# Six weight slots in the in-projection rounds; x leaves the chip after the first norm and is loaded again

## The chip, the cores and the metric

The kernel runs on one core of one Trainium2 chip. The metric is the device time of one execution in microseconds (us), the median of several runs. The activations, the weights and the result are float32; large products are made of rounded high and low parts, as told below.

## The reference

One decoder layer on 256 tokens of width 2048: a norm, one wide projection (16 heads of mLSTM and retention with their gates), the heads, an output projection, and a dense feed-forward block. Cut to what matters here:

```python
h = rmsnorm(x, g_mix_pre[l])                       # (256, 2048)
proj = h @ w_in[l]                                 # w_in: 2048 x 8208
mq, mk, mv, mo, mi, mf, rq, rk, rv, rg = jnp.split(proj, SPLITS, axis=-1)
qk = jax.nn.silu(causal_dwconv(jnp.concatenate([mq, mk], axis=-1), conv_w[l], conv_b[l]))
hm = mlstm_chunkwise(...)                          # 8 heads, chunks of 128
hm = head_rmsnorm(hm, g_mlstm_head[l]) * jax.nn.sigmoid(mo)
hr = retention_chunkwise(rotary(rq), rotary(rk), rv)   # 8 heads
hr = head_rmsnorm(hr, g_ret_head[l]) * jax.nn.silu(rg)
mix = jnp.concatenate([hm, hr], axis=-1) @ w_out[l]    # 2048 x 2048
x = x + rmsnorm(mix, g_mix_post[l])
h = rmsnorm(x, g_ffn_pre[l])
ff = (jax.nn.silu(h @ w_gate[l]) * (h @ w_up[l])) @ w_down[l]   # width 5632
x = x + rmsnorm(ff, g_ffn_post[l])
```

## The kernel before

**Weights.** All weights stream through `raw`, four chunks of 1 MB (`RAW_CHUNKS`), filled by SyncE's DMA queue. A piece of 1024 columns of a chunk (a "sub"; eight subs are a "round", two subs fill a chunk) is converted by ScalarE into a rounded high part (`hi`, L711, into `w_hi`), VectorE makes the low part from the raw value and the high part (`lo`, L1132, into `w_lo`), and TensorE multiplies with both (`sub_columns`, `sub_tokens`, all through `mm` at L1787). `w_hi` and `w_lo` have `AHEAD` = 4 slots each. `more_hi` and `more_lo` are two further slots each, so that the feed-forward rounds have `FF_SLOTS` = 6. They lie in the same on-chip memory as `resid`, which holds x from the start of the kernel to the end of the output projection.

**Rounds.** Four rounds (0 to 3) make the values v. Then come twelve in-projection rounds, `R_IN` = 4 to 15. In this text they are rounds P0 to P11, and their subs are counted through, sub 0 to sub 95: P0 has subs 0 to 7, P1 has 8 to 15, P7 has 56 to 63, P8 has 64 to 71. They go in groups of three, one group for four heads: a query round, a key round (`KEY_ROUNDS`: P1, P4, P7, P10) and a gate round. During the gate round TensorE also does the heads of the group: `scores`, `weighted`, `turned`. A round has two units, each with its own pair of accumulator banks. Four output-projection rounds (`R_OUT`) follow.

**What sets the order.** The order on each engine is written out by hand. "Step n" is what ScalarE and VectorE do once TensorE has finished sub n (`sub_done`). In step n ScalarE converts sub n + 4 (`ahead`, then `hi`), and VectorE makes its low part (`lo`). Between the conversions stand the mixer's pieces (`mixer_step`, `head_step`): at the end of a unit ScalarE copies half of the accumulators into `right` (`copy_right`, L828), VectorE adds the other half (`unit_sums`, L1319), which also tells TensorE that the banks are free (`acc_free`), and then does a convolution in two halves (`convolve`, L1342 and L1346) or, in the third and fourth group, a rotation (`rotate`, L1356 to L1362). ScalarE then makes `qT` or `kT` (L867) for `scores`. VectorE's `weigh` (L1374) turns the scores into `probs` for `weighted`. Once, in P1, ScalarE also makes the decay matrices of the first eight heads (`mlstm_decay`, L818 to L822), from a row that goes through main memory by the POOL queue (`neg_all`). In most steps the conversion stands ahead of the mixer's piece; in steps 3, 5 and 7 of a key round it stands behind it on ScalarE.

**Loads.** `load` waits until VectorE has made the low parts of all subs of the chunk's former contents (`lo_done`), then issues the transfer; `raw_full` tells ScalarE of its landing. In the key rounds the source is cut so that a contiguous piece of main memory is 256 columns, 1 KB; in the other in-projection rounds it is 2 KB.

## Time and profile before

| | us |
|---|---|
| median of 3 runs (1198.7 to 1198.92) | 1198.8 |
| the profiled execution, its device time | 1198.35 |
| its span, first to last instruction | 1196.6 |

| engine | busy us | share of the span |
|---|---|---|
| TensorE (PE) | 1183.2 | 99% |
| VectorE (DVE) | 997.0 | 83% |
| ScalarE (ACT) | 690.6 | 58% |
| GpSimd (POOL) | 81.4 | 7% |

The granted TensorE clock is full in all 40 slices. The weights make 231.05 MB on SyncE's queue, whose packets take 61.9% of the 16 DMA engines' time. Read such a page from the engine that is never idle: here TensorE, so that only what makes TensorE wait, or adds work to it, moves the time. Busy times of matmuls overlap and hide short waits, so the waits are read from start times in the timeline.

### The profile page before, as it was taken

What the parts mean: (1) busy time and instruction counts of PE and PEld (TensorE: products, weight loads), DVE (VectorE), ACT (ScalarE), POOL (GpSimd) and SP (SyncE); (2) the same over time, 40 slices, a digit from 0 to 9 for tenths busy, and PEclk for the clock granted to TensorE, in tenths of its full rate; (3) what the DMA queues carried; (4) which work ended last, traced back from release to release, by engine and by line L of the source; (5) the groups of instructions that cost most, each with busy time, mean ns of one, the idle gap of its engine ahead of it and who ended that gap; (6) DMA issues with size and microseconds to landing.
All of it is one profiled execution on the core that took longest, in us unless ns stands there. A gap on an engine that the chain in (4) does not pass through costs nothing.

```text
span 1196.6 us, 16463 instructions
## 1 busy us (share of the span) xinstructions
PE 1183.2 (99%) x5727; PEld 992.7 (83%) x5727; DVE 997.0 (83%) x1334; ACT 690.6 (58%) x930; POOL 81.4 (7%) x87
## 2 busy tenths in 40 slices
PE   8999999999999999999999999999999999999997
PEld 7888888888888888888888888888888888888885
DVE  6656777877786755879999999999999789979997
ACT  5654676474654744665666566555656455555553
POOL 1000110000000000001110110111010011001100
PEclk9999999999999999999999999999999999999999
DMA  8656867767786656565575666657566765655654
GB/s 314 206 159 158 226 172 153 182 144 190 182 190 170 226 186 194 171 236 195 198 234 184 205 212 221 200 192 238 185 201 210 246 199 192 217 201 188 231 170 149
DMA packets 124596, 237.23 MB, mean 198 GB/s; under 512 B 8312, under 2 KB 24960, under 8 KB 123392
## 3 DMA queue, kind: packets, MB, share of 16 engines
q1 hardware_dynamic: 122784, 231.05, 61.9%
q0 software_dynamic: 1760, 5.51, 1.8%
q8 instruction: 30, 0.49, 0.2%
q14 instruction: 22, 0.18, 0.0%
HBM read 229.97 MB, written 4.20 MB: 196 GB/s over the span
## 4 chain that ended last, share of the span: by engine, by line
PE 92%; DVE 4%; DMA 2%; ACT 1%; issue 1%; SPq 0%; DVEq 0%; ACTq 0%
PE bank L1787 90%; DMA raw<-in_w_in 2%; DVE w_lo L1132 1%; DMA resid<-in_x 1%; PE bank L2064 1%; DVE w_lo L1618 0%; PE bank L1792 0%; PE bank L1981 0%; ACT w_hi L711 0%; DVE more_lo L1618 0%; DVE raw L1635 0%; DVE v_sb L1259 0%; DVE gT L1346 0%; DVE h L1159 0%; DVE resid L1780 0%
## 5 line engine op out<-in xcount | busy, mean ns | idle before, releaser
L1132 DVE TENSOR_TENSOR w_lo<-raw,w_hi 128x1024 fp32r<-128x1024 f32 x172 | 209.1, 1223 | 120.4 <-ACT w_hi L711 120.0
L711 ACT ACTIVATE w_hi<-raw 128x1024 fp32r<-128x1024 f32 x172 | 180.5, 1058 | 162.0 <-PE bank L1787 149.6
L1787 PE MATMUL bank<-hT,w_hi 128*128 128x512 f32 x768 | 271.1, 396 | 0.4 <-DVE w_lo L1132 0.4
L1787 PE MATMUL bank<-w_hi,h2T 128*128 128x512 f32 x778 | 253.4, 391 | 0.0
L1787 PE MATMUL bank<-hT,w_lo 128*128 128x256 f32 x768 | 214.6, 279 | 0.0
L1787 PEld LDWEIGHTS bank<-hT,w_hi 128*128 128x128 f32 x768 | 144.0, 187 | 32.7 <-DVE w_lo L1132 0.7
L1787 PEld LDWEIGHTS bank<-w_hi,h2T 128*128 128x128 f32 x778 | 146.1, 188 | 30.0
L1787 PE MATMUL bank<-w_lo,h2T 128*128 128x512 f32 x379 | 147.5, 389 | 0.0
L1787 PEld LDWEIGHTS bank<-hT,w_lo 128*128 128x128 f32 x768 | 145.0, 189 | 0.0
L1615 DVE TENSOR_TENSOR w_lo<-raw,w_hi 128x1024 fp32r<-128x1024 f32 x108 | 131.0, 1228 | 12.6 <-ACT w_hi L1022 12.5
L1618 DVE TENSOR_TENSOR w_lo<-raw,w_hi 128x1024 fp32r<-128x1024 f32 (+1 forms) x130 | 135.2, 1075 | 2.3 <-ACT w_hi L1036 1.7
L1036 ACT ACTIVATE w_hi<-raw 128x1024 fp32r<-128x1024 f32 (+1 forms) x130 | 115.8, 934 | 36.3 <-PE bank L1787 22.3
L1787 PE MATMUL bank<-w_hi,ffT 128*128 128x512 f32 x406 | 129.6, 389 | 0.0
L1022 ACT ACTIVATE w_hi<-raw 128x1024 fp32r<-128x1024 f32 x108 | 109.6, 1051 | 33.9 <-PE bank L1787 33.1
L1036 ACT ACTIVATE more_hi<-raw 128x1024 fp32r<-128x1024 f32 x78 | 74.7, 975 | 54.7 <-DVE raw L1630 45.5
L671 POOL TENSOR_TENSOR raw<-raw 128x512 f32<-128x512 f32 x43 | 60.1, 1399 | 545.6 <-DVE w_lo L1615 177.4
L1787 PEld LDWEIGHTS bank<-w_hi,ffT 128*128 128x128 f32 x406 | 76.2, 188 | 15.8
L1618 DVE TENSOR_TENSOR more_lo<-raw,more_hi 128x1024 fp32r<-128x1024 f32 x78 | 88.1, 1143 | 1.0
L1787 PE MATMUL bank<-more_hi,h2T 128*128 128x512 f32 x258 | 85.8, 389 | 0.0
L1787 PEld LDWEIGHTS bank<-w_lo,h2T 128*128 128x128 f32 x379 | 71.2, 188 | 14.5
L1787 PE MATMUL bank<-w_hi,hT 128*128 128x512 f32 x256 | 81.3, 393 | 1.0 <-DVE w_lo L1132 1.0
L1787 PE MATMUL bank<-w_hi,mixT 128*128 128x512 f32 x256 | 80.1, 391 | 0.0
(265 smaller groups left out, 1819.5 us busy)
## 6 DMA issues: line engine op xcount, KB each, us to landing
raw<-in_w_in SPq DMA_DIRECT2D x63, 1024.0 KB, 11.0
raw<-in_w_down SPq DMA_DIRECT2D x88, 512.0 KB, 4.9
raw<-in_w_up SPq DMA_DIRECT2D x80, 512.0 KB, 3.9
raw<-in_w_gate SPq DMA_DIRECT2D x80, 512.0 KB, 4.7
raw<-in_w_out SPq DMA_DIRECT2D x16, 1024.0 KB, 5.1
raw<-in_w_gate SPq DMA_DIRECT2D x4, 1024.0 KB, 5.2
raw<-in_w_up SPq DMA_DIRECT2D x4, 1024.0 KB, 6.7
raw<-raw POOLq DMA_DIRECT2D x9, 256.0 KB, 5.8
```

The costliest lines, as they stand in the source:

```text
L671: pool.tensor_tensor(b12, b22, b12, ALU.subtract).then_inc(t3_ready, 1)
L711: act.activation(part_of(w_hi, rnd, s), src, ACT.Copy).then_inc(hi_done, 1)
L1022: act.activation(hi_slots[slot], raw[:, q, SUB * piece:SUB * (piece + 1)], ACT.Copy).then_inc(hi_done, 1)
L1036: act.activation(slot_blocks(hi_slots, slot, piece), seven_blocks(piece, q), ACT.Copy).then_inc(hi_done, 1)
L1132: dve.tensor_tensor(part_of(w_lo, rnd, s), raw_sub(rnd, s)[1], part_of(w_hi, rnd, s).bitcast(F32), ALU.subtract).then_inc(lo_done, 1)
L1615: dve.tensor_tensor(lo_slots[slot], raw[:, q, SUB * piece:SUB * (piece + 1)], hi_slots[slot].bitcast(F32), ALU.subtract).then_inc(lo_done, 1)
L1618: dve.tensor_tensor(slot_blocks(lo_slots, slot, piece), seven_blocks(piece, q), slot_blocks(hi_slots, slot, piece).bitcast(F32), ALU.subtr ...
L1787: return pe.matmul(out_, lhsT, rhs, start=start, stop=stop, skip_group_check=True)
L2064: ins = pe.transpose(bank[:, b0 + j // 2, c:c + P], ff(t)[:, j * P:(j + 1) * P], ident)
```

## The change

The in-projection rounds use all six slots. `in_slot` gives the slot of a sub of these rounds, `next_ahead` the sub that is converted in a step: n + 6 where it was n + 4. ScalarE and VectorE convert subs 4 and 5 before the loop over the rounds, after waiting until x has been read by the first norm (`h_ready`, `sq_done`). In the last two steps of the last round nothing is converted, and the output projection goes on with four slots. Since `more_hi` and `more_lo` overwrite x, SyncE loads x again into `resid`, behind the loads of the second output round, and VectorE waits for it (`x_again`) before the residual is added.

```diff
+def in_slot(rnd, s):
+    if isinstance(rnd, int) and R_IN <= rnd < R_OUT:
+        return (8 * (rnd - R_IN) + s) % FF_SLOTS
+    return s % AHEAD
+
+def next_ahead(rnd, s):
+    if not R_IN <= rnd < R_OUT:
+        return s + AHEAD
+    return s + FF_SLOTS if (rnd, s) < (R_OUT - 1, 8 - (FF_SLOTS - AHEAD)) else None
...
-            with sp.Fori(1, 4) as g:
+            for g in range(1, 4):
                 for q in range(4):
                     load(g + R_OUT, q, rows(w_out, 4 * q, 4, 512 * g, 512))
+                if g == 1:
+                    sp.wait_ge(sub_done, 8 * R_OUT)
+                    for t in range(TT):
+                        sp.dma_start(resid[:, t, :], x[0, t * P:(t + 1) * P, :]).then_inc(x_again, 16)
...
             def ahead(rnd, s):
                 act.wait_ge(sub_done, 8 * rnd + s + 1)
-                hi(rnd, s + AHEAD)
+                following = next_ahead(rnd, s)
+                if following is not None:
+                    hi(rnd, following)
...
             gate_rows()
+            act.wait_ge(h_ready, CHUNKS * TT)
+            act.wait_ge(sq_done, XP * TT)
+            for s in range(AHEAD, FF_SLOTS):
+                hi(R_IN, s)
             for rnd in range(R_IN, R_OUT):
...
+            dve.wait_ge(h_ready, CHUNKS * TT)
+            for s in range(AHEAD, FF_SLOTS):
+                lo(R_IN, s)
             for rnd in range(R_IN, R_OUT):
                 for s in range(8):
...
-                        lo(rnd, s + AHEAD)
+                        ahead_lo(rnd, s)
                     else:
-                        lo(rnd, s + AHEAD)
+                        ahead_lo(rnd, s)
                         mixer_step(rnd, s)
...
             dve.wait_ge(acc_free, E_FF + 1)
+            dve.wait_ge(x_again, 16 * TT)
             last_columns(mixed, g_post1, Q_POST1, 0, V_POST1, 1)
...
                 pe.wait_ge(lo_done, 8 * rnd + s + 1)
-                slot = s % AHEAD
+                slot = in_slot(R_IN + kind, s)
```

The first place is ScalarE from the first conversion after the gate rows to the copy at the end of P0. `raw_full1` is the landing of the chunk with subs 10 and 11, `raw_full2` of subs 12 and 13, `raw_full3` (the last row) of subs 14 and 15. Before:

```order
L711 ACTIVATE w_hi<-raw 128x1024 [waits raw_full3,sub_done]
L711 ACTIVATE w_hi<-raw 128x1024 [waits raw_full0,sub_done] x2
L828 ACTIVATE right<-bank 128x512 [waits acc_free]
L711 ACTIVATE w_hi<-raw 128x1024 [waits raw_full1,sub_done] x2
L867 ACT_TABLE_LOAD
L867 ACTIVATE qT<-pre 128x512 [waits tiles_done]
L828 ACTIVATE right<-bank 128x512 [waits acc_free]
L711 ACTIVATE w_hi<-raw 128x1024 [waits raw_full2,sub_done] x2
```

After:

```order
L730 ACTIVATE w_hi<-raw 128x1024 [waits raw_full3,sub_done]
L730 ACTIVATE w_hi<-raw 128x1024 [waits raw_full0,sub_done] x2
L730 ACTIVATE more_hi<-raw 128x1024 [waits raw_full1,sub_done] x2
L849 ACTIVATE right<-bank 128x512 [waits acc_free]
L730 ACTIVATE w_hi<-raw 128x1024 [waits raw_full2,sub_done] x2
L888 ACT_TABLE_LOAD
L888 ACTIVATE qT<-pre 128x512 [waits tiles_done]
L849 ACTIVATE right<-bank 128x512 [waits acc_free]
L730 ACTIVATE w_hi<-raw 128x1024 [waits raw_full3,sub_done] x2
```

The copy into `right` of P0's first unit now stands behind the conversions of subs 10 and 11, and the copy of the second unit behind those of subs 12 and 13.

The second place is ScalarE in the key round of the third group (P7): the copies of its two units, and the conversions of P8's chunks around them. Before:

```order
L828 ACTIVATE right<-bank 128x512 [waits acc_free,sub_done]
L711 ACTIVATE w_hi<-raw 128x1024 [waits raw_full3,sub_done]
L711 ACTIVATE w_hi<-raw 128x1024 [waits raw_full0,sub_done]
L867 ACTIVATE kT<-pre 128x512 [waits tiles_done,sub_done]
L711 ACTIVATE w_hi<-raw 128x1024 [waits raw_full1,sub_done]
L711 ACTIVATE w_hi<-raw 128x1024 [waits raw_full0,sub_done]
L828 ACTIVATE right<-bank 128x512 [waits acc_free,sub_done]
L711 ACTIVATE w_hi<-raw 128x1024 [waits raw_full2,sub_done]
L711 ACTIVATE w_hi<-raw 128x1024 [waits raw_full3,sub_done]
```

After:

```order
L849 ACTIVATE right<-bank 128x512 [waits acc_free,sub_done]
L730 ACTIVATE more_hi<-raw 128x1024 [waits raw_full1,sub_done]
L730 ACTIVATE w_hi<-raw 128x1024 [waits raw_full0,sub_done]
L888 ACTIVATE kT<-pre 128x512 [waits tiles_done,sub_done]
L730 ACTIVATE w_hi<-raw 128x1024 [waits raw_full2,sub_done]
L730 ACTIVATE w_hi<-raw 128x1024 [waits raw_full3,sub_done]
L849 ACTIVATE right<-bank 128x512 [waits acc_free,sub_done]
L730 ACTIVATE w_hi<-raw 128x1024 [waits raw_full1,sub_done]
```

The second copy (of the key round's second unit) stood ahead of the first conversions out of P8's chunks 2 and 3; it now stands behind both.

The third place is VectorE after the gate rows. The five rows L1299 to L1303 end in the row for `neg_all`. Before:

```order
L1132 TENSOR_TENSOR w_lo<-raw,w_hi 128x1024 [waits hi_done,gates_dve]
L1132 TENSOR_TENSOR w_lo<-raw,w_hi 128x1024 [waits hi_done]
L1299 COPY h<-h 8x256
L1300 TENSOR_TENSOR h<-h 8x256 [waits gates_dve]
L1301 SCALAR_TENSOR_TENSOR h<-h 8x256 [waits gates_dve]
L1302 TENSOR_SCALAR h<-h 8x256 [waits gates_dve]
L1303 SCALAR_TENSOR_TENSOR h<-h 8x256 [waits gates_dve]
L1132 TENSOR_TENSOR w_lo<-raw,w_hi 128x1024 [waits hi_done,gates_dve]
```

After:

```order
L1157 TENSOR_TENSOR more_lo<-raw,more_hi 128x1024 [waits hi_done,h_ready,gates_dve]
L1157 TENSOR_TENSOR more_lo<-raw,more_hi 128x1024 [waits hi_done]
L1157 TENSOR_TENSOR w_lo<-raw,w_hi 128x1024 [waits hi_done] x2
L1324 COPY h<-h 8x256
L1325 TENSOR_TENSOR h<-h 8x256 [waits gates_dve]
L1326 SCALAR_TENSOR_TENSOR h<-h 8x256 [waits gates_dve]
L1327 TENSOR_SCALAR h<-h 8x256 [waits gates_dve]
L1328 SCALAR_TENSOR_TENSOR h<-h 8x256 [waits gates_dve]
```

The low parts of subs 6 and 7 now come ahead of the five gate rows, where they came behind them.

## Rows read from the trace of the kernel before

**Rows 1.** The page, part 4: the chain that ended last, by engine.

```profile
PE 92%; DVE 4%; DMA 2%; ACT 1%; issue 1%; SPq 0%; DVEq 0%; ACTq 0%
```

**Rows 2.** Waits of TensorE, whole span: total us, times, longest us.

```profile
PE bank L1787 <- DVE w_lo L1132: 1.4, 3, 0.6
PE bank L1787 <- ACT kT L867: 0.6, 1, 0.6
```

**Rows 3.** Timeline of TensorE: start us, us, engine, line, operation, tiles, forms, [idle before].

```profile
129.46 0.40 PE L1787 MATMUL bank<-hT,w_hi 128*128 128x512 f32 x1
...
149.82 0.50 PE L1787 MATMUL bank<-hT,w_hi 128*128 128x512 f32 x1 [0.42 <-DVE w_lo L1132]
...
153.53 0.48 PE L1787 MATMUL bank<-qT,kT 128*128 128x256 f32 x1 [0.62 <-ACT kT L867]
```

**Rows 4.** Timeline of ScalarE, steps 5 to 13 of the in-projection.

```profile
124.60 0.60 ACT L828 ACTIVATE right<-bank 128x512 f32<-128x512 f32 x1
126.32 1.06 ACT L711 ACTIVATE w_hi<-raw 128x1024 fp32r<-128x1024 f32 x1 [1.12 <-PE bank L1787]
...
140.30 1.06 ACT L711 ACTIVATE w_hi<-raw 128x1024 fp32r<-128x1024 f32 x1 [0.74 <-DMA raw<-in_w_in]
141.38 1.28 ACT L818 ACT_TABLE_LOAD   x1
...
144.88 0.58 ACT L828 ACTIVATE right<-bank 128x512 f32<-128x512 f32 x1
...
152.85 0.63 ACT L867 ACTIVATE kT<-pre 128x512 f32<-128x512 f32 x1
```

**Rows 5.** SyncE's issue of P1's chunk 1, its us to landing; chunk 3 in the chain.

```profile
105.68 0.37 SPq L527 DMA_DIRECT2D raw<-in_w_in  x1
...
raw<-in_w_in SPq DMA_DIRECT2D x1, 1024.0 KB, 20.6
...
121.70 18.52 DMA raw<-in_w_in
```

**Rows 6.** Timeline of VectorE, steps 2 to 11.

```profile
119.18 2.36 DVE L1132 TENSOR_TENSOR w_lo<-raw,w_hi 128x1024 fp32r<-128x1024 f32 x2
...
125.86 0.69 DVE L1319 TENSOR_TENSOR pre<-bank,right 128x512 f32<-128x512 f32 x1
...
130.69 0.88 DVE L1346 SCALAR_TENSOR_TENSOR pre<-pre,columns,gT 128x256 f32<-128x256 f32 x2
...
145.49 0.69 DVE L1319 TENSOR_TENSOR pre<-bank,right 128x512 f32<-128x512 f32 x1 [2.87 <-ACT right L828]
```

**Rows 7.** Stretches: busy us by engine (instructions), clock, DMA share, GB/s last.

```profile
120.00:125.00 5.00, 5.00 (x31) 4.35 (x30) 3.16 (x4) 2.52 (x3) 0.00 (x0) 1.00 0.71 139
...
135.00:140.00 5.00, 5.00 (x30) 4.34 (x29) 5.00 (x10) 1.70 (x2) 0.00 (x0) 1.00 0.95 311
...
290.00:310.00 20.00, 20.00 (x120) 17.66 (x119) 14.03 (x18) 9.02 (x11) 0.00 (x0) 1.00 0.72 209
```

**Rows 8.** Timelines of ScalarE, VectorE and TensorE, end of P7 and start of P8.

```profile
300.25 0.60 ACT L828 ACTIVATE right<-bank 128x512 f32<-128x512 f32 x1 [0.70 <-PE bank L1787]
...
308.67 2.01 ACT L711 ACTIVATE w_hi<-raw 128x1024 fp32r<-128x1024 f32 x2 [4.74 <-DMA raw<-in_w_in]
...
303.66 0.55 DVE L1374 SCALAR_TENSOR_TENSOR probs<-bank,decay 128x384 f32<-128x384 f32 x1
...
296.21 0.37 SPq L527 DMA_DIRECT2D raw<-in_w_in  x1
...
306.36 0.49 PE L1787 MATMUL bank<-v_sb,probs 128*128 x3
```

**Rows 9.** Output projection: w_out's issues; the third round's first issue and conversion.

```profile
raw<-in_w_out SPq DMA_DIRECT2D x16, 1024.0 KB, 5.1
...
420.96 0.37 SPq L527 DMA_DIRECT2D raw<-in_w_out  x1
...
437.83 1.06 ACT L711 ACTIVATE w_hi<-raw 128x1024 fp32r<-128x1024 f32 x1 [1.66 <-PE bank L1787]
```

More of the change, by code:

```diff
@@ L397, in part_of @@
         def part_of(w, rnd, s):
-            part = w[:, s % AHEAD, :]
+            part = w[in_slot(rnd, s)]
             return part.rearrange("p (k c) -> p k c", c=256) if wide_order(rnd) else part
@@ L447, in hybrid_layer @@
         resid_back = sem("resid_back")
+        x_again = sem("x_again")
         h_ready = sem("h_ready")
@@ L710, in hi @@
                     act.wait_ge(raw_full[chunk], 16 * (rnd + 1))
[L711 removed]
+                act.activation(part_of(hi_slots, rnd, s), src, ACT.Copy).then_inc(hi_done, 1)
             def early_hi(s):
@@ L1131, in lo @@
                 dve.wait_ge(hi_done, 8 * rnd + s + 1)
-                dve.tensor_tensor(part_of(w_lo, rnd, s), raw_sub(rnd, s)[1],
-                                  part_of(w_hi, rnd, s).bitcast(F32), ALU.subtract).then_inc(lo_done, 1)
+                dve.tensor_tensor(part_of(lo_slots, rnd, s), raw_sub(rnd, s)[1],
+                                  part_of(hi_slots, rnd, s).bitcast(F32), ALU.subtract).then_inc(lo_done, 1)
             def early_lo(s):
@@ L1434, in mixer_step, with ahead_lo @@
                             (convolve if group < 2 else rotate)(group, part, u, half)
+            def ahead_lo(rnd, s):
+                following = next_ahead(rnd, s)
+                if following is None:
+                    dve.wait_ge(sub_done, 8 * rnd + s + 1)
+                else:
+                    lo(rnd, following)
+            dve.wait_ge(h_ready, CHUNKS * TT)
+            for s in range(AHEAD, FF_SLOTS):
+                lo(R_IN, s)
             for rnd in range(R_IN, R_OUT):
@@ L1805, in sub_columns @@
                         cols = slice(256 * j + P * c, 256 * j + P * (c + 1))
-                        mm(bank[:, 2 * pair + c, :], w_hi[:, slot, cols], act_T[:, k, :], k == 0, False)
-                        ins = mm(bank[:, 2 * pair + c, 0:SEQ], w_lo[:, slot, cols], act_T[:, k, 0:SEQ],
+                        mm(bank[:, 2 * pair + c, :], hi_slots[slot][:, cols], act_T[:, k, :], k == 0, False)
+                        ins = mm(bank[:, 2 * pair + c, 0:SEQ], lo_slots[slot][:, cols], act_T[:, k, 0:SEQ],
                                  False, k == KT - 1)
@@ L1817, in unit_columns @@
                         before(s)
-                    sub_columns(rnd, s, act_T, unit, q)
+                    sub_columns(rnd, s, act_T, unit, q, 1)
                     if after:
@@ L1828, in wide_columns @@
                         before(s)
-                    sub_columns(rnd, s, act_T, u, q)
+                    sub_columns(rnd, s, act_T, u, q, 0 if order is QUERY_ORDER else 2)
                     if after:
```

3 lines of the change are left out of this document (1 added, 2 removed).

## The prediction, made before the changed kernel was run

> **What bounds the kernel now.** I read the chain by engine first: 92% of it is TensorE [rows 1], so the kernel is as long as TensorE's work plus its waits. The change takes no product away and adds none; it can only move waits. So next come TensorE's waits. For weights (`w_lo`, made by VectorE) it waits three times, 1.4 us in all, and for `kT` once, 0.6 us [rows 2]. Its timeline shows where in the in-projection this is [rows 3]: 149.82, at the last sub of P1, on weights, and 153.53, at the first head of P2, on `kT`. After 160 us the largest wait of TensorE up to the output projection is a fraction of a microsecond. All that two more slots can win by themselves is therefore some 2 us, 0.2% of the time. Then I read what else is queued on ScalarE and VectorE in these rounds, since their instructions are done in order, and a conversion that waits for its transfer holds up the mixer's pieces behind it. That is the question here.
>
> **Part 1: the conversion goes two subs further, from P0 on.** In step n ScalarE now converts sub n + 6. It asks for the raw data two subs, some 5.6 us, earlier (the first head of P2 follows eight subs behind sub 8, in 153.53 - 129.46 = 24.1 us with about a microsecond of waits in it [rows 3], so a sub takes 2.8 to 2.9). Loads are issued when low parts are done, so wherever conversions really come two subs earlier, so do the loads, and nothing is lost. But at the start of P0 they do not. P1's chunk 1 (subs 10 and 11) is issued at 105.68, when VectorE is done with sub 3, the same instant in both kernels, and takes 20.6 us [rows 5]: it lands at 126.3. Before, that was just in time: step 6 converted sub 10 at 126.32 and had nothing urgent behind it [rows 4]. Now step 4, at about 120.6 (three subs and a few transposes before 129.46), asks for it, and behind it in step 5 stands the copy into `right` of P0's first unit, which ran at 124.60 [rows 4]. TensorE needs what VectorE makes of this copy (`unit_sums`, done before at 125.86 + 0.69 [rows 6]) for its free banks at sub 8, at 129.46 [rows 3].
>
> Worked out: conversions of subs 10 and 11 from 126.3, 2.0 us for two that follow each other [rows 8], to 128.3; the copy, while VectorE makes the two low parts, 2.4 us from 127.4 [rows 6], to 129.8; the sum 0.69 [rows 6], to 130.5. Sub 8 starts 1.0 us late. **First term: a new wait of 1.0 us.** It does not add to the end if a later wait is fixed by something else, and it is.
>
> That something is the chain that ended in `kT` at 152.85. Before, ScalarE waited until 140.30 for P1's chunk 3 (subs 14 and 15), issued at 121.70 and 18.52 us on the way [rows 4, 5]; then table load and three heads' decay matrices, 3.5 us, and the copy of P1's first unit at 144.88 [rows 4]; `kT` came 8.0 us after that copy. Everything from this copy on is the same list of instructions after the change. So the term is how much later this copy is. Two things can set it:
> - VectorE's own backlog. From 129.8 it has, back to back: for each of P0's two units the sum, the scaling and the first half of the convolution, 0.7 + 0.7 + 0.7 + 0.8 = 2.9 us, and the second half, 1.6 (two pairs of 0.88 that overlap a little [rows 6]), so 9.0 in all; between them the low parts of subs 12, 13 and 14, 1.14 each when they follow on other work, 3.4; gate columns 0.2. 129.8 + 9.0 + 3.4 + 0.2 = 142.4. Then ScalarE's `qT` 0.6, one conversion 1.0, and the 3.5 from before: 147.5. That is 2.6 us later than 144.88.
> - The landing of chunk 3, which stands ahead of the second unit's convolution. If it stays at 140.2, then conversion 1.1, low part 1.2, second half 1.7, `qT` 0.6, conversion 1.0, 3.5: 149.3, or 4.4 us later. It may come earlier, since its load is issued when VectorE is done with sub 7, and that low part now stands ahead of the five gate rows, which take the 2.2 us between 116.9 and 119.18: issued at 119.4, it could land at 137.9, and then the backlog decides. The transfers before it are slow (139 GB/s while up to 311 is reached later [rows 7]), so an earlier request does find room; but chunk 1 is in the way until 126.3.
>
> **Second term: TensorE reaches the first head of P2 2.6 to 4.4 us later, and the first term and both old waits of this place are contained in it.** I take 3.5, the middle, as I have no reason for either end. The wait on weights at 149.82 does go, as the change intends, but TensorE then waits that much longer for `kT`.
>
> The Trainium skill, in PSUM — Partial Sum Buffer, Engine vs sequencer instructions, says that the queues of ScalarE and VectorE are strictly first in, first out. The rows at 140.30 to 144.88 agree: everything behind the late chunk waited [rows 4].
>
> **Part 2: the same in P7 and P8.** Here the transfers are slow again: ScalarE waited 4.74 us until 308.67 for P8's chunk 3, issued at 296.21 [rows 8]. Before, the copy of P7's second unit was ahead of this in the queue, at 300.25, and `probs` of the first head were ready at 303.66 + 0.55 = 304.2, 2.2 us before TensorE wanted them at 306.36 [rows 8]. Now the copy is behind both of P8's late chunks. If chunk 3 lands at L, `probs` are ready at L + 1.0 (conversion) + 1.2 (low part) + 3.4 (sum, rotation and weighing, 304.2 less the end of the copy, 300.8), and TensorE wants them at 306.36 + 3.5 = 309.9. The load of chunk 3 waits for the low part of P7's last sub. That now comes two subs earlier against TensorE, 2 us earlier by the clock since all is 3.5 later, and it leaves a step in which a first half of a rotation, 3 us, stands ahead of it; so L lies between 308.6 - 5 = 303.6 and 308.6. The wait lies between 0 (309.2 against 309.9) and 4.3 us. **Third term: 1.5 us.** I choose nearer the lower end, since the transfers moved 209 GB/s here against 311 elsewhere [rows 7]: there is room for a request that comes earlier.
>
> In the other groups (P4, P10) ScalarE does not wait for transfers before the change, and loads move with the conversions there; I cost them at nothing. What hides it is the time that a chunk lies landed; if that were gone, each would cost like P7.
>
> **Part 3: x leaves and returns.** Conversions into the extra slots wait for x to be read by the first norm, long over at 113 us. The second load of x is 2 MB. A megabyte of `w_out` takes 5.1 us [rows 9], so x takes about 10.2. In the worst case all of it stands ahead of the third output round's first chunk, issued at 420.96: 420.96 + 10.2 + 5.1 = 436.3, and that chunk is first converted at 437.83 [rows 9]. The cover is 1.5 us on ScalarE and four slots, some 11 us, on TensorE. SyncE's new wait (`sub_done` at the end of the in-projection) is over when it comes to it, as the loads ahead of it waited for low parts of later subs. VectorE's `x_again` is over some 50 us before it is asked for. Cost nothing. The loop on SyncE written out is as many issues. The last two steps of P11 have no conversion: nothing waits there.
>
> **Sum.** 3.5 + 1.5 = 5.0 us later. Against the profiled execution: 1198.35 + 5.0 = 1203.35. That execution is 0.45 us under the median, so 1203.8.
>
> **Rivals.**
> - *The slots do what they are for* (faster). P1's chunk 1 lands before 120.6, for example because the loads behind it are asked for earlier; then no copy is held up, and weights at 149.82 and `kT` at 153.53 come in time, about 1.9 us less: 1196.9. Against it: the load was issued before the two kernels differ. The Trainium skill's rule, in Perfetto Trace Analysis, Optimization Strategy, points this way: repeated gaps on the engine that should be full can mean too few buffers. The trace does not agree: the gaps are two, not repeated, and both go back to the same late transfer. Chance 0.06.
> - *The delay is taken up on the way.* Chunks 2 and 3 land 3 us or more earlier and VectorE overlaps better than I add up; TensorE is late by only the 1.0 of the first term, and P8's copy is in time: 1199.8. It decides at a landing of chunk 3 before about 135. Chance 0.17.
> - *The transfers are the bound in both places* (slower still). Chunk 3 of P1 stays at 140.2 and P8's chunk 3 at 308.6: 4.4 + 3.4 (`probs` at 314.2, wanted at 306.36 + 4.4 = 310.8) = 7.8, and 1206.6; with x in the way of w_out by a microsecond, 1207.6. Chance 0.15.
> - *My forecast*, 1201.4 to 1206: chance 0.62.
>
> **How the numbers follow.** The lower bounds of both terms give 2.6 + 0 = 2.6: 1201.4. The range goes down to 1200.4, into the second rival, and up to 1207.0, which leaves out the first rival, most of the second and the tail of the third, about 0.2. A measurement of this kernel can tell 0.2%, 2.4 us, from no change. Faster by more than that: the tail of the first rival, 0.05. Slower: nearly all of the forecast and all of the third rival, 0.75. The rest, 0.2, within.
>
> **What would show it.** Right: ScalarE idle before the conversion of sub 10, until about 126.3, on a transfer; the first copy near 128.5; a start of sub 8 near 130.5 with idle time before it; `scores` of P2 at 156 to 158, waiting for `kT`; a wait for `probs` near 310; no wait of TensorE for `w_lo` around 150. Wrong: the conversion of sub 10 before 122, or sub 8 at 129.5; or a wait in the output projection, near 436 us, which would be the second load of x.

## The result, and the profile after

| | us |
|---|---|
| after, median of 5 executions (1204.62 to 1208.88) | 1206.39 |
| before, beside it, median of 5 (1197.99 to 1200.46) | 1198.8 |
| ratio, 95% interval | 1.0063 [1.0048, 1.0079] |
| the profiled execution of after, its device time | 1204.62 |
| its span | 1202.9 |

The changed kernel is slower by 7.6 us. The profiled execution is the fastest of its five; it is 6.27 us longer than the profiled one of before (1198.35).

First the waits of TensorE over the whole span (total us, times, longest us). These answer to [rows 2]; of after, the four that matter:

```profile
PE bank L1824 <- ACT kT L888: 5.2, 1, 5.2
PE bank L1824 <- issue: 1.5, 1, 1.5
...
PE bank L1824 <- DVE pre L1344: 0.9, 1, 0.9
PE bank L1824 <- DVE w_lo L1157: 0.8, 2, 0.4
```

The wait for `kT` has grown from 0.6 to 5.2 us. The waits for `w_lo` have gone from three to two; they had 1.4 us in all, now 0.8. Both that are left stand in the first 100 us, ahead of the in-projection, where before has two of its three (1.0 us in all); the one that is gone is the 0.42 us at 149.82. Two small ones are new, one for `pre` and one named "issue". The timeline of TensorE says where they are; it answers to [rows 3]:

```profile
130.47 0.50 PE L1824 MATMUL bank<-hT,w_hi 128*128 128x512 f32 x1 [0.86 <-DVE pre L1344]
...
149.99 0.39 PE L1824 MATMUL bank<-hT,w_hi 128*128 128x512 f32 x1
...
158.08 1.65 PE L1824 MATMUL bank<-qT,kT 128*128 128x256 f32 x4 [5.15 <-ACT kT L888]
159.38 0.77 PE L1824 MATMUL bank<-hT,more_hi 128*128 128x512 f32 x1
...
165.78 0.38 PE L1824 MATMUL bank<-v_sb,probs 128*128 x2
...
406.25 0.47 PE L1824 MATMUL bank<-w_hi,mixT 128*128 128x512 f32 x1
```

Sub 8 starts at 130.47, 1.01 us late. Sub 15 starts at 149.99 without a wait, as the change intends. The scores of P2's first head start at 158.08 and not at 153.53, 4.55 us late. The first weighted product of P2 stands at 165.78. The timeline of before has it at 160.32, and the first product of the output projection at 401.29:

```profile
160.32 0.48 PE L1787 MATMUL bank<-v_sb,probs 128*128 x2 [0.31 <-DVE probs L1374]
...
401.29 0.47 PE L1787 MATMUL bank<-w_hi,mixT 128*128 128x512 f32 x1
```

So another 0.9 us was lost between 158 and 166 us, where TensorE did not wait: the four score products took 1.65 us where four take 0.92 at full clock (in before at 153.53 and in the profile with the filling products, below). At the start of the output projection the distance is 4.96 us (406.25 - 401.29), half a microsecond less than the 5.46 at 160.32. The two timelines show where it went: 0.1 us in the products up to 161.66, 0.2 at the head at 313.34 in before, and 0.2 in products that run slightly slower in before from 314 to 327 us. Nothing here shows that the change has to do with it.

The chain on ScalarE that ends in `kT`, from its timeline of after, answers to [rows 4]; the last line is from VectorE's:

```profile
126.23 2.01 ACT L730 ACTIVATE more_hi<-raw 128x1024 fp32r<-128x1024 f32 x2 [7.13 <-PE bank L1824]
128.27 0.60 ACT L849 ACTIVATE right<-bank 128x512 f32<-128x512 f32 x1
131.30 2.01 ACT L730 ACTIVATE w_hi<-raw 128x1024 fp32r<-128x1024 f32 x2 [2.43 <-DMA raw<-in_w_in]
...
140.38 2.01 ACT L730 ACTIVATE w_hi<-raw 128x1024 fp32r<-128x1024 f32 x2 [3.81 <-DMA raw<-in_w_in]
144.32 0.64 ACT L888 ACTIVATE qT<-pre 128x512 f32<-128x512 f32 x1 [1.93 <-DVE pre L1371]
144.86 1.05 ACT L730 ACTIVATE more_hi<-raw 128x1024 fp32r<-128x1024 f32 x1
145.93 1.28 ACT L839 ACT_TABLE_LOAD   x1
...
149.43 0.58 ACT L849 ACTIVATE right<-bank 128x512 f32<-128x512 f32 x1
...
157.40 0.63 ACT L888 ACTIVATE kT<-pre 128x512 f32<-128x512 f32 x1
...
141.48 1.23 DVE L1157 TENSOR_TENSOR w_lo<-raw,w_hi 128x1024 fp32r<-128x1024 f32 x1 [1.87 <-ACT w_hi L730]
```

Read from below: `kT` comes 8.0 us after the copy at 149.43, as in before after the copy at 144.88. The copy stands behind the table load and three heads' decay matrices. Before, this table load was at 141.38, right behind the conversion of sub 14. Now there stand between them the conversion of sub 15, a wait of 1.93 us for VectorE, `qT` and the conversion of sub 16: 145.93 - 141.38 = 4.55 us, exactly the lateness of the scores. And the conversion of sub 14 itself starts at 140.38, when its chunk has landed, as in before at 140.30. VectorE's line says which of the two bounds of the prediction held: its backlog was done 1.87 us before the low part of sub 14 could be made, so the landing of chunk 3 set the time. Without that wait the lateness would have been, as an estimate, 4.55 - 1.87 = 2.7 us, the prediction's lower bound of 2.6. (The first row of ScalarE, 126.23, waited for a chunk as well: it had to wait for TensorE only until about 120.6. The releaser that is named came first, and had long been done.)

### The profile page after: what moved, and what is told of

Same layout as the page of the kernel before. It is cut to its first block, busy times and chain, and to the rows that moved or that the text cites. A ratio compares the mean times of both kernels' runs of the same rounds, so it can differ in the third digit from the quotient of the medians.

```text
span 1202.9 us, 16428 instructions
## 1 busy us (share of the span) xinstructions
PE 1182.7 (98%) x5727; PEld 992.7 (83%) x5727; DVE 998.6 (83%) x1334; ACT 691.3 (57%) x930; POOL 82.3 (7%) x87
## 4 chain that ended last, share of the span: by engine, by line
PE 90%; DVE 4%; DMA 3%; ACT 1%; issue 1%; SPq 0%; POOL 0%; DVEq 0%; ACTq 0%
PE bank L1824 88%; DMA raw<-in_w_in 3%; DVE w_lo L1157 1%; DMA resid<-in_x 1%; PE bank L2101 1%; DVE w_lo L1655 0%; PE bank L1829 0%; PE bank L2018 0%; ACT w_hi L730 0%; DVE more_lo L1655 0%; DVE v_sb L1284 0%; DVE raw L1672 0%; DVE w_lo L1652 0%; DVE more_lo L1157 0%; DVE h L1184 0%
## 5 line engine op out<-in xcount | busy, mean ns | idle before, releaser
L1157 DVE TENSOR_TENSOR w_lo<-raw,w_hi 128x1024 fp32r<-128x1024 f32 x140 | 170.4, 1224 | 101.7 <-ACT w_hi L730 101.1
L730 ACT ACTIVATE w_hi<-raw 128x1024 fp32r<-128x1024 f32 x140 | 147.0, 1060 | 134.2 <-PE bank L1824 121.9
L1824 PE MATMUL bank<-hT,w_hi 128*128 128x512 f32 x512 | 180.2, 395 | 0.9 <-DVE pre L1344 0.9
L1824 PE MATMUL bank<-hT,w_lo 128*128 128x256 f32 x512 | 142.8, 279 | 0.0
L1652 DVE TENSOR_TENSOR w_lo<-raw,w_hi 128x1024 fp32r<-128x1024 f32 x108 | 131.1, 1230 | 12.6 <-ACT w_hi L1047 12.5
L1047 ACT ACTIVATE w_hi<-raw 128x1024 fp32r<-128x1024 f32 x108 | 109.7, 1053 | 33.8 <-PE bank L1824 33.6
L1824 PEld LDWEIGHTS bank<-hT,w_hi 128*128 128x128 f32 x512 | 95.9, 187 | 22.2 <-DVE pre L1344 1.2
L1824 PEld LDWEIGHTS bank<-hT,w_lo 128*128 128x128 f32 x512 | 96.6, 189 | 0.0
L1824 PE MATMUL bank<-hT,more_hi 128*128 128x512 f32 x256 | 91.6, 400 | 0.0
```

The source lines that it names most:

```text
L730: act.activation(part_of(hi_slots, rnd, s), src, ACT.Copy).then_inc(hi_done, 1)
L1047: act.activation(hi_slots[slot], raw[:, q, SUB * piece:SUB * (piece + 1)], ACT.Copy).then_inc(hi_done, 1)
L1157: dve.tensor_tensor(part_of(lo_slots, rnd, s), raw_sub(rnd, s)[1], part_of(hi_slots, rnd, s).bitcast(F32), ALU.subtract).then_inc(lo_done, 1)
L1652: dve.tensor_tensor(lo_slots[slot], raw[:, q, SUB * piece:SUB * (piece + 1)], hi_slots[slot].bitcast(F32), ALU.subtract).then_inc(lo_done, 1)
L1824: return pe.matmul(out_, lhsT, rhs, start=start, stop=stop, skip_group_check=True)
```

## The experiments

All comparisons are with runs of the kernel before on the same chip (medians 1198.1 to 1198.64 us).

| kernel | median us | ratio to before, 95% |
|---|---|---|
| x alone | 1198.18 | 1.0001 [0.9992, 1.001] |
| lead of six from P3 on | 1199.92 | 1.0014 [1.0005, 1.0023] |
| lead of six from P2 on | 1199.11 | 1.0008 [0.9999, 1.0017] |
| lead of five | 1201.19 | 1.0025 [1.0014, 1.0035] |
| filled wait | 1203.98 | 1.0051 [1.0037, 1.0065] |
| after, again | 1206.52 | 1.0067 [1.0048, 1.0085] |
| chunk 1 in wide rows | 1199.59 | 1.0013 [1.0004, 1.0022] |
| chunk 3 in wide rows | 1204.8 | 1.0055 [1.0042, 1.0069] |
| all chunks in wide rows | 1203.63 | 1.0049 [1.0035, 1.0062] |
| before, all in wide rows | 1197.79 | 0.999 [0.9981, 0.9999] |
| after, mixer's pieces first | 1208.16 | 1.0075 [1.0058, 1.0091] |
| before, mixer's pieces first | 1201.46 | 1.0018 [1.0009, 1.0028] |

### x alone

```diff
 def in_slot(rnd, s):
-        return (8 * (rnd - R_IN) + s) % FF_SLOTS
+        return s % AHEAD
 def next_ahead(rnd, s):
-    return s + FF_SLOTS if (rnd, s) < (R_OUT - 1, 8 - (FF_SLOTS - AHEAD)) else None
+    return s + AHEAD
...
-            for s in range(AHEAD, FF_SLOTS):
-                hi(R_IN, s)
```

> After, but the in-projection goes back to four weight slots; x still leaves the chip with the first norm and is loaded again in the output projection. Theory A (the loss comes wholly from the conversions made two ahead, which delay the mixer's copies of P0 to P2): the time is that of before, 1198.8 us within 0.8, and TensorE's waits near sub 8 (0) and at P2's first head (0.6 us, ending near 153.5 us) read as in before. Theory B (the second load of x, or the unrolled issue of loads, costs something that the traces hide): 1200 to 1204 us, with a wait in the output projection or the loss near 975 us still there. The 1.1 us that after loses just ahead of the down projection, near 975 us, is expected to be gone if it belongs to the slots' larger lead, and to stay if it belongs to the layout of the program.

The time is that of before, to 0.1 us, and TensorE waits 0.55 us for `kT` at 152.45. The second load of x costs nothing. In after, too, TensorE has no wait between 400 and 450 us, where the 2 MB pass. The median from issue to landing is 8.1 us, over all four transfers of x (two at the start of the kernel, two here) and over the two here alone:

```profile
resid<-in_x SPq DMA_DIRECT2D x4, 1024.0 KB, 8.1
```

Theory A holds: the whole loss is in the lead of six. The wait of 1.1 us near 975 us is absent too, but that says little, as told under the clock.

### Where the lead is built up

Two kernels keep the six slots, but run four subs ahead at first and make the two extra conversions later, at the end of P2 or of P1:

```diff
 def next_ahead(rnd, s):
+    if rnd < R_IN + 3:
+        return s + AHEAD
...
-            for s in range(AHEAD, FF_SLOTS):
-                hi(R_IN, s)
...
+                    if rnd == R_IN + 2 and s == 7:
+                        for more in range(AHEAD, FF_SLOTS):
+                            hi(R_IN + 3, more)
```

(and the same for `lo`; with R_IN + 2, R_IN + 1 and R_IN + 2 in the other).

> After with its six slots, but the loads and conversions are four subs ahead until P2's last step, where the two extra conversions are made; from P3 on they are six ahead. Theory A (only the two extra conversions ahead of the mixer's pieces of P0 and P1 cost time): 1198.8 us within 0.8, no wait of TensorE over 1 us at P2's first head, the span 5 us below after's. Theory B (six slots cost time by themselves, wherever the lead is built up): the loss stays, 1202 to 1206 us, and a new wait stands near P3 or P4. Gain below before: at most 1 us, from the 0.28 us and 0.4 us waits of before near 288 and 313 us.

> After with its six slots, but four subs ahead until P1's last step, where the two extra conversions are made; six ahead from P2 on. With the extra conversions a round later, at the end of P2, the kernel had 1199.9 us. Theory A (the mechanism is a late chunk with copies behind it, and it holds in P2 as well as in P1, since P2's chunk 3 landed at 157.2 us in before, only 0.1 us ahead of its conversion): the wait ahead of the scores of P2 is below 1.5 us, and a wait of 2 to 4.5 us for the weighting in P2 appears near 162 us, behind P2's chunk 3; 1201 to 1204 us. Theory B (only P0 and P1 suffer, since there the gates' rows and decay matrices are made too): 1198.5 to 1200.5 us.

Built up at the end of P2: 1199.92, and the wait at P2's first head is 0.62 us, as in before. That is 1.75 us above before and clear of the noise, so the expected 1198.8 within 0.8 was missed by a little. The profiled execution has one wait of its own. First the timeline of VectorE, then that of TensorE:

```profile
184.99 2.35 DVE L1160 TENSOR_TENSOR more_lo<-raw,more_hi 128x1024 fp32r<-128x1024 f32 x2
...
188.04 0.61 DVE L1428 TENSOR_SCALAR y<-bank,stat 128x128 f32<-128x128 f32 x2
```

```profile
188.71 0.44 PE L2022 MATMUL bank<-columns,y 128*128 128x128 f32 x2 [0.88 <-DVE y L1428]
```

The two extra low parts stand in the queue ahead of `y`, for which TensorE waits (in before `y` is made at 186.00): extra conversions cost what they hold up. These 0.88 us are half of the difference; the rest is not explained. Built up at the end of P1: 1199.11, which can't be told from before. Theory A of this run, a wait of 2 to 4.5 us behind P2's chunk 3, falls: there are only 0.31 and 0.49 us for `probs`. Its trace shows why: ScalarE does wait for P2's chunk 3 (0.64 us, until 157.10), but the copy of P1's second unit ran at 154.94, ahead of that conversion. So six slots by themselves cost little, and they gain nothing that can be measured: neither kernel beats before.

### Lead of five

```diff
-    return s + FF_SLOTS if (rnd, s) < (R_OUT - 1, 8 - (FF_SLOTS - AHEAD)) else None
+    return s + 5 if (rnd, s) < (R_OUT - 1, 7) else None
...
-            for s in range(AHEAD, FF_SLOTS):
-                hi(R_IN, s)
+            hi(R_IN, AHEAD)
```

> After with its six slots, but loads and conversions run five subs ahead in the in-projection, not six (one extra conversion ahead of P0, not two). Theory A (the loss grows with how far a conversion stands ahead of the copies, because P1's chunk 3 is asked for a step earlier with each sub of lead while it lands at 140.3 us): TensorE's wait ahead of the scores of P2 is 1.5 to 4 us, between the 0.6 us of four and the 5.2 us of six, and the time is 1200 to 1204 us. Theory B (six is special, because conversions then come in pairs that wait for one chunk): the wait is below 1 us and the time that of before, 1198.6 us.

The timeline of ScalarE, and then TensorE's scores of P2's first head:

```profile
126.49 1.06 ACT L730 ACTIVATE more_hi<-raw 128x1024 fp32r<-128x1024 f32 x1 [4.74 <-DMA raw<-in_w_in]
...
140.12 1.06 ACT L730 ACTIVATE w_hi<-raw 128x1024 fp32r<-128x1024 f32 x1 [3.47 <-DMA raw<-in_w_in]
...
143.08 1.28 ACT L839 ACT_TABLE_LOAD   x1
```

```profile
155.23 1.65 PE L1822 MATMUL bank<-qT,kT 128*128 128x256 f32 x4 [2.76 <-ACT kT L888]
```

Four subs ahead the wait is 0.62 us, five 2.76, six 5.15, and the table load stands at 141.38, 143.08 and 145.93, while chunk 3 lands at the same time in all three. Theory A: a conversion that is asked for earlier, with its chunk landing when it did, only shifts copies behind itself.

### Wide rows: which transfer it is

In the key rounds the source is cut into pieces of 1 KB. These four kernels load such chunks in pieces of 2 KB, as in the other rounds; the key rounds then multiply other weights, as the expectations say.

```diff
-                            if n == 1:
+                            if n == 1 and q != 1:
                                 src = in_rows(8 * (q % 2), 8, col + (q // 2) * 256, 256)
```

(q != 3 for chunk 3; the branch is left out for all chunks, in after and in before).

> After, but the weights of the key rounds (P1, P4, P7, P10) are loaded with rows of 2 KB as those of every other round, in place of rows of 1 KB. Their order in the slot is then another, so these rounds multiply other weights: the amount of work is the same, the result isn't. Theory A (what makes the conversion of sub 10, and with it everything that stands behind it on ScalarE, late is P1's chunk 1, which took 20.6 us to land in before): chunk 1 lands several us earlier, TensorE's wait ahead of P2's first head falls from 5.2 us below 1.5 us, and the time is 1197 to 1200 us. Theory B (ScalarE and VectorE simply have too much to do in P0 and P1): chunk 1's landing changes little for the wait, which stays over 4 us, and the time is 1204 to 1206 us.

> Before, with the weights of the key rounds (P1, P4, P7, P10) loaded with rows of 2 KB in place of 1 KB. These rounds then multiply other weights; the amount of work is the same, the result isn't. With six slots the wider rows brought P1's chunk 1 down from 126.2 to 116.3 us and took 2.8 us off the median, and a new wait of 3.6 us for the weighting in P2 appeared, behind P2's chunk 3 that landed at 157.5 us. Theory A (that new wait belongs to the conversion's place six subs ahead): with four slots it is absent, and the time is 1197 to 1198.2 us. Theory B (the wider rows themselves push P2's loads back): a wait of 1 to 4 us for the weighting near 160 us here too, 1199 to 1202 us.

> After, with chunk 1 alone of each key round loaded with rows of 2 KB (the key rounds then multiply other weights; the amount of work is the same, the result isn't). All key rounds' chunks in wide rows took 4 of the 5.2 us wait ahead of the scores of P2. Theory A (what counts is chunk 3, whose landing at 140.3 us holds the last copies of P1's second and third unit): chunk 3 still lands near 140 us, the wait stays 4 to 5 us, only the 1.0 us at sub 8 goes, 1204 to 1206 us. Theory B (what counts is chunk 1, which starts the backlog at 126.2 us): the wait falls below 2.5 us, 1201 to 1204 us.

> After, with chunk 3 alone of each key round loaded with rows of 2 KB (other weights in the key rounds, the same amount of work, another result). Theory A (chunk 3's landing counts): it lands before 138 us, and TensorE's wait ahead of the scores of P2 falls by about as much as it lands earlier, to 1 to 3 us; the 1.0 us at sub 8 stays; 1202 to 1204.5 us. Theory B (chunk 1 counts): the wait stays 4 to 5 us, 1205 to 1207 us. If chunk 3 does not land earlier, because it is queued behind chunk 1, the run tells only that.

Chunk 1 alone in wide rows takes 6.8 us off after's time (1206.4 to 1199.59), more than either theory of that run had expected, and leaves waits of 0.9 us for `kT` and 1.1 us for `probs`. ScalarE with chunk 1 in wide rows:

```profile
121.46 1.06 ACT L730 ACTIVATE more_hi<-raw 128x1024 fp32r<-128x1024 f32 x1 [2.03 <-DMA raw<-in_w_in]
...
124.33 0.60 ACT L849 ACTIVATE right<-bank 128x512 f32<-128x512 f32 x1
...
126.25 1.06 ACT L730 ACTIVATE w_hi<-raw 128x1024 fp32r<-128x1024 f32 x1 [1.32 <-DMA raw<-in_w_in]
...
132.90 1.06 ACT L730 ACTIVATE w_hi<-raw 128x1024 fp32r<-128x1024 f32 x1
...
140.75 1.28 ACT L839 ACT_TABLE_LOAD   x1
```

Chunk 1 lands 5 us earlier, at 121.4, and chunks 2 and 3, which are still cut into 1 KB, land 5 and 7.5 us earlier (126.2 and 132.8 for 131.2 and 140.3): they were queued behind it. The copy that sub 8 waits for comes at 124.33, the table load at 140.75. With chunk 3 alone in wide rows the conversion of sub 14 starts at 139.14, 1.2 us earlier, and the wait at the scores is still 4.1 us, beside one of 1.9 us at sub 8: chunk 3 was still behind chunk 1. The scores start at 158.30, no earlier than in after. In that execution chunk 1 landed at 127.0, 0.9 us later than in after; VectorE came to the low part of sub 14 at 140.67 without a wait, so that now its backlog decided; and the conversion of sub 16 waited another 0.80 us, for P2's first chunk. An earlier landing of chunk 3 alone thus gains little, as the backlog that starts with chunk 1 stands close behind it. So chunk 1 is the root, as theory B of that run says. What the two runs do not tell apart is by which way it acts, by its own late landing at 126.2 or by the landing of chunk 3 that goes with it; that in after it is the second, by 1.87 us over the first, is read from the chain above, not from an experiment.

With all chunks in wide rows the wait for `kT` is 1.2 us, but a new one of 3.6 us appears, in the timelines of ScalarE and of TensorE:

```profile
157.56 1.06 ACT L727 ACTIVATE w_hi<-raw 128x1024 fp32r<-128x1024 f32 x1 [3.02 <-DMA raw<-in_w_in]
158.52 0.58 ACT L846 ACTIVATE right<-bank 128x512 f32<-128x512 f32 x1
```

```profile
163.38 0.93 PE L1821 MATMUL bank<-v_sb,probs 128*128 x6 [3.56 <-DVE probs L1396]
```

The same thing one round later: the conversion of sub 20 waits for P2's chunk 3, the copy of P1's second unit waits behind it, and `probs` are late. My expectation, 1197 to 1200, had not thought of it. In before with wide rows this wait of TensorE is absent (1197.79, theory A). ScalarE waits for P2's chunk 3 there as well, 2.86 us, until 158.67; but four subs ahead the copy of P1's second unit stands in front of that conversion, at 154.29, and nothing urgent waits. That is the clearest sign that the order in the queue costs, and not the late chunk by itself. 1197.79 is also the one gain of this study, 0.1%, at the edge of what its interval can tell, and it needs another arrangement of the weights in main memory to give the right result.

### The mixer's pieces first

```diff
-                    if rnd in KEY_ROUNDS and s in (3, 5, 7):
+                    if rnd in KEY_ROUNDS and s in (3, 5, 7) or rnd < R_IN + 2:
...
-                    if rnd == R_IN + 1 and 2 <= s < 5:
-                        for h in range(3 * s - 6, min(3 * s - 3, HEADS)):
+                    if rnd == R_IN + 1 and 3 <= s < 6:
+                        for h in range(3 * s - 9, min(3 * s - 6, HEADS)):
```

(and the first edit on VectorE).

> After, but in P0 and P1 ScalarE and VectorE do each step's piece of the mixer ahead of the conversion of the sub six on, and the decay matrices are made one step later. Nothing is computed otherwise. Theory A (it is the order in the two queues, a conversion that waits for a late chunk with the copies behind it, that costs after its 7.6 us): the keys of P2 are ready in time, TensorE's wait ahead of the scores of P2 falls from 5.2 us below 1 us, the wait at sub 8 goes, and the time is 1197 to 1199.5 us. Theory B (the two extra conversions are simply too much work for P0 to P2, in whatever order): the wait only moves, 1203 to 1206 us. If a wait for w_lo appears near sub 14 (chunk 3 of P1 lands at 140.3 us, and sub 14 is due at 146 us), up to 2 us of the gain go to it.

> Before (four slots, x kept on the chip), with the same reordering as in the run with the mixer's pieces first. With four slots the conversion of sub 15 was ready only 0.05 us ahead of TensorE in before, so each piece of the mixer put ahead of a conversion can make TensorE wait. Theory A (what six slots are good for is to let the mixer's pieces go first): waits for w_lo of 1 to 4 us in P1, 1199 to 1202 us, and so at least 1 us more than with six slots. Theory B (four slots are enough for either order): 1197.5 to 1198.8 us.

The first expectation was missed on both sides: 1208.16, the slowest kernel of all. The second kernel, at 1201.46, lies in the range of its theory A, 1199 to 1202, but by luck: the waits for `w_lo` in P1 that were to make it slower are not there, and it is 6.7 us faster than with six slots, not slower. The wait at sub 8 has gone, but TensorE waited longer than in after at the scores, and not for `kT`. The timelines of TensorE, of after with this order and of before with it:

```profile
163.09 1.64 PE L1824 MATMUL bank<-qT,kT 128*128 128x256 f32 x4 [10.16 <-ACT decay L843]
```

```profile
154.98 1.43 PE L1787 MATMUL bank<-qT,kT 128*128 128x256 f32 x3 [2.85 <-ACT decay L822]
```

`scores` waits for all decay matrices too (`decay_ready`, L1997), and I had moved these a step later together with the order. So the times have two causes in them and say nothing on the order alone. The timelines of ScalarE tell a little more. With four slots and this order `kT` is begun at 150.35, 2.5 us earlier than in before (152.85), and what TensorE waits for is the moved decay matrices alone. With six slots `kT` is begun only at 158.47 and the last decay matrix ends 3.8 us after `kT` does; so some 6 of the 10.16 us would be there without the move. But in that execution chunk 2 of P1 landed at 136.4, 5.2 us later than in after at the same time of issue; why is open. Whether a better order of these queues would let six slots pay was not settled.

### The clock

> After, with 20 matmuls of 512 columns that nobody reads, put behind P1's last sub, where TensorE otherwise sits idle for 5.2 us ahead of the scores of P2. They should fill about 4.5 us of that wait. Theory A (part of the loss is that TensorE runs its next work at half clock once it has sat idle): the granted clock stays at 1.0 from 155 to 162 us, the scores of P2 take 0.9 us and not 1.65, sub 16 starts 0.8 to 1.2 us earlier than in after, and the median is 1203 to 1205 us with runs closer to one another than after's 1204.6 to 1208.9. Theory B (the clock is chance and costs nothing): 1206 us as after. The wait for P2's keys itself ends at 158 us in both.

> After, unchanged, on the chip and in the hours of the experiments, with a second profile. The first profile is of its fastest execution: 1204.6 us at a mean granted clock of 0.997, the other four had 0.995 and 1205.9 to 1208.9 us. Theory A (the loss varies with how long TensorE runs at half clock behind its 5.2 us wait): an execution at a mean clock of 0.995 shows 3 to 4 us more at half clock near 158 to 165 us, beside the tail of 6.3 us, and the median lies again 2 to 3 us above the 1204.0 us of the kernel with the filling matmuls. Theory B (those four were chance): the median is that of the kernel with filling matmuls within 0.8 us. The loss of 1.1 us near 975 us is expected in about one of two profiles.

The edit of the first, in TensorE's program behind P1's last unit:

```diff
+            for _ in range(20):
+                mm(bank[:, B_T, :], hT[:, 0, 0:P], hT[:, 0, :], True, True)
```

Stretches of the profile (busy us by engine, TensorE first, then the granted clock, DMA share, GB/s) from 155 us on, of after, of after again, and of the kernel with the filling products:

```profile
155.00:158.00 3.00, 0.00 (x0) 0.00 (x0) 2.25 (x4) 2.26 (x5) 2.41 (x4) 0.93 0.12 46
158.00:161.00 3.00, 2.92 (x9) 2.54 (x10) 1.99 (x2) 3.00 (x5) 0.00 (x0) 0.50 0.66 182
161.00:164.00 3.00, 3.00 (x19) 2.61 (x18) 2.93 (x7) 1.15 (x2) 0.00 (x0) 1.00 0.45 170
```

```profile
155.00:158.00 3.00, 0.00 (x0) 0.00 (x0) 2.56 (x5) 2.24 (x4) 2.71 (x5) 0.84 0.06 21
158.00:161.00 3.00, 2.61 (x8) 2.24 (x9) 1.69 (x2) 3.00 (x5) 0.00 (x0) 0.50 0.58 146
161.00:164.00 3.00, 3.00 (x11) 2.59 (x10) 2.93 (x6) 0.66 (x1) 0.00 (x0) 0.52 0.55 206
```

```profile
155.00:158.00 3.00, 2.50 (x12) 1.72 (x10) 2.84 (x5) 2.24 (x5) 2.99 (x6) 1.00 0.09 36
158.00:161.00 3.00, 2.33 (x13) 2.11 (x14) 1.41 (x2) 3.00 (x5) 0.00 (x0) 1.00 0.49 122
```

The last one's timeline of TensorE:

```profile
152.76 4.74 PE L1824 MATMUL bank<-hT 128*128 128x512 f32 x20
158.67 0.92 PE L1824 MATMUL bank<-qT,kT 128*128 128x256 f32 x4 [1.17 <-ACT kT L888]
```

With TensorE idle for 5.15 us (5.09 in the second profile) its clock goes to 0.50, that is 1.2 in place of 2.4 GHz, and it stays there for the first 2.9 us of new work in one execution and for some 5.5 in the other; the first weighted product comes at 165.78 in the one, 167.25 in the other, though the scores started at 158.08 and 158.39: behind the scores the clock costs 0.9 us in the one and 2.1 in the other, against the 6.79 us that before takes for the same stretch. With 4.74 us of the wait filled the clock stays at 1.00. The scores themselves started later, at 158.67, as `kT` came 0.6 us later; in that execution P1's chunk 3 was converted from 140.97 on, 0.6 us later than in after. So sub 16 is not earlier (159.34 for 159.38), which I had expected. Yet the median is 1203.98, against 1206.39 and 1206.52 for after: some 2.4 us of the loss are the clock. The intervals of the ratios overlap, but the slowest of the five executions (1204.69) is level with the fastest of after's eleven (1204.58). In this both theories A hold. The time at half clock, twice what the clock lacks to 1.00, is 0.4 + 3.0 = 3.4 us from 155 to 164 in the first profile of after and 1.0 + 3.0 + 2.9 = 6.9 in the second, 3.5 more. The Trainium skill, in TensorE: Matmul & The Clock Gate, Part 1: The HAM clock gate, says that the throttled state is the default and activity is what releases it; the rows agree.

The lead of five shows that the clock can cost as much as the wait: its scores were 1.70 us late (155.23), and its first weighted product, at 164.34 for 160.32, 4.0 us. Here TensorE was idle for 2.76 us only, and the granted clock was 0.50 from 155 to 161 us.

The 1.1 us at 975 us, last. In both kernels that are compared first there is a wait for "issue" ahead of the first down product, 0.41 in before and 1.51 us in after; in the second profile of after it is 0.48. Over the fourteen profiles of this study it is 0.4 to 0.6 in nine and 1.3 to 1.5 in five, each time with GpSimd idle 10.1 to 11.1 us for a chunk of `w_down` in place of 9.2 to 9.5. One of the five is a kernel with four slots (before with the mixer's pieces first), and after itself has it in one profile and not in the other: it goes with how the transfers fall in one execution. Whether the change makes it more frequent is not shown.

## Why the prediction was right, and where it was off

The range, 1200.4 to 1207.0, holds 1206.39, the sign is right, and the mechanism is the one forecast. The time taken, 1203.8, is 2.6 us short, and the forecast's own span, 1201.4 to 1206, is missed by 0.4. By its steps:

- **First term, sub 8 late by 1.0 us.** Right to a tenth: conversion from 126.23, copy 128.27, sub 8 at 130.47, worked out as 130.5.
- **Second term, 2.6 to 4.4 us, taken 3.5.** It was 4.55 (4.86 in the second profile). The upper bound was "the landing of chunk 3, if it stays at 140.2", and it stayed: 140.3. I let the request that comes earlier count in favour of an earlier landing. It was issued at about 119.3, 2.4 us earlier, and landed at the same time, behind chunk 1. "I take the middle, as I have no reason for either end" was the mis-sized step, and there was a reason for the upper one: the prediction itself says that chunk 1 is in the way until 126.3, and chunk 3 stands behind it in the same queue. With the landing where it was, the sum of the upper bound, 149.3 for the copy, is right to 0.15 us (149.43).
- **Third term, 0 to 4.3 us, taken 1.5.** It was 0, and the sign that was named for it, a wait for `probs` near 310, is not there. P8's chunk 3 was issued at 292.09, 4.1 us earlier than before (296.21 [rows 8]), and took 10.1 us where it had taken 12.4: it landed at 302.2, earlier than my lower bound of 303.6. The copy ran when TensorE released it, and `probs` were ready 2.2 us ahead of TensorE, as before. The timelines of ScalarE, VectorE and TensorE of after:

```profile
305.62 0.60 ACT L849 ACTIVATE right<-bank 128x512 f32<-128x512 f32 x1 [1.71 <-PE bank L1824]
...
309.00 0.55 DVE L1399 SCALAR_TENSOR_TENSOR probs<-bank,decay 128x384 f32<-128x384 f32 x1
...
311.73 0.83 PE L1824 MATMUL bank<-v_sb,probs 128*128 x6
```

- **The second load of x: nothing.** Right, and shown by the kernel that does that part alone.
- **What the sum left out: the clock.** 0.9 us in the profiled execution, some 2.4 us in the median. A forecast wait of four microseconds on an engine that otherwise never stops should have been costed with it. The profile of before had no such case but at its end, where the granted clock is 1.00 from 1190 to 1193 us and 0.61 from there to 1196.6, with the last product at 1188.
- **What the slots could win at most.** The prediction has some 2 us and counts all three waits for `w_lo`, but two of them, 1.0 of the 1.4 us, stand ahead of the in-projection, where nothing changed. Only 0.42 + 0.62 = 1.0 us was within reach, so the first rival's 1196.9 was too low from the start.

The profiled execution adds up: 4.55 (scores late) + 0.9 (clock) - 0.5 (made up until the output projection, above) + 1.1 (the down projection's chunk, chance) = 6.05 of 6.27. My sum, 5.0, came near it by a term too small, one too large and one left out. That the range holds the median owes something to this: the width allowed for P8 covered what the clock took.

Of the rivals, *transfers are the bound in both places* had the time, 1206.6, but only half of its mechanism: in P1 the transfer was the bound, in P8 it was not, and the clock filled the place. *The delay is taken up* and *the slots do what they are for* fell with the landings at 140.3 and 126.2. The condition of the latter, chunk 1 landing before 120.6, was met in the kernel with all chunks in wide rows (116.3), and nearly (121.4) with chunk 1 alone in wide rows; no copy of P0 was held up then, and even so six slots gained nothing (1203.63 and 1199.59).

## What to carry to other kernels

More buffers let a consumer ask earlier; they do not make a transfer land earlier, and where queues are in order, a conversion that waits for its data takes the urgent pieces behind it along. A late chunk with the urgent copy ahead of it cost nothing here (before with wide rows). Before deepening a prefetch, list for each late transfer what will then stand behind its consumer, and look for the slow transfer at the head of the queue: here one chunk cut into 1 KB pieces set the landing of the two behind it. And cost a long wait of TensorE with the half clock behind it, up to as much again.

## What the runs showed of the hardware

**Rows of 1 KB.** While chunks 0 and 1 of P1 are under way, after (1 KB pieces) and the kernel with all chunks in 2 KB pieces, 107 to 112 us and, in after alone, 115 to 118:

```profile
107.00:112.00 5.00, 5.00 (x31) 4.39 (x30) 4.71 (x11) 1.75 (x5) 0.00 (x0) 1.00 0.89 121
...
115.00:118.00 3.00, 3.00 (x20) 2.61 (x19) 3.00 (x4) 3.00 (x4) 0.00 (x0) 1.00 0.44 96
```

```profile
107.00:112.00 5.00, 5.00 (x31) 4.34 (x30) 4.70 (x12) 1.75 (x5) 0.00 (x0) 1.00 1.02 244
```

Half the rate at nearly the same share of busy DMA engines, 121 against 244 GB/s. With chunk 1 alone in 2 KB pieces the same stretch still moves 116 GB/s, and the rate rises only from 115 us on (183, where after has 96). And for the last third of chunk 1's transfer, with the next loads not yet issued, only 0.44 of the engines' time is busy. The Trainium skill, in Perfetto Trace Analysis, DMA Optimizations, says that transfers under 2 KB carry a significant overhead each. It speaks of transfers; here each transfer is 1 MB and what is under 2 KB is its contiguous piece. Read so the rows agree, with a factor of two. It is not so everywhere: from 124 to 127 us before moves 292 GB/s, with P1's chunks in 1 KB pieces under way and P2's first, in 2 KB pieces, issued only at 126.0. What makes the difference is open.

**VectorE behind GpSimd.** In three of the five profiles with the late `w_down` chunk, GpSimd's subtraction began just ahead of a small sum of VectorE. Of after, and the same sum in its second profile:

```profile
975.27 1.97 POOL L690 TENSOR_TENSOR raw<-raw 128x512 f32<-128x512 f32 x1 [10.84 <-DMA raw<-in_w_down]
...
976.00 1.38 DVE L1759 TENSOR_TENSOR d_sum<-d_sum,d_whole 128x128 f32<-128x128 f32 x1
```

```profile
977.63 0.28 DVE L1759 TENSOR_TENSOR d_sum<-d_sum,d_whole 128x128 f32<-128x128 f32 x1
```

0.28 us become 1.38, and the sum ends 0.14 us after GpSimd does (977.24 and 977.38). The Trainium skill, in SBUF — State Buffer, SBUF: two separate sides, says that the two share a port pair which one holds alone for a whole instruction, against an instruction of VectorE with two inputs from this memory; the rows agree. The sum can't be the whole of that 1 us wait of TensorE, since two further profiles have 1.28 and 1.38 us of it with the sum at 0.28.
